# Finishing u one chunk later in the SwiGLU groups of a two-block fp32 transformer kernel, spreading the token sums, and reordering seven products

## The reference, cut to what matters

```python
def _sq_relu_mlp(h, w_up, w_down):          # first block, D_FF = 4096: stages "f0", "f1"
    u = jax.nn.relu(h @ w_up)
    return (u * u) @ w_down

def swiglu(x, w_gu, w_d):                   # second block, D_FF_2 = 2816: "s00", "s01", "s10", "s11"
    gate, up = jnp.split(x @ w_gu, 2, axis=-1)
    return (jax.nn.silu(gate) * up) @ w_d
```

## Time and profile before

| | |
|---|---|
| median of 3 runs | 3586.6 us (3584.88 to 3589.55) |
| profiled execution, its own time | 3591.5 us |
| its span | 3589.8 us |
| TensorE, VectorE, ScalarE, GpSimd busy | 96%, 65%, 40%, 26% of the span |
| mean granted TensorE clock | 0.987 |

### The profile page before, as it was taken

How to read it: one execution, slowest core, us unless ns; L and a number is a source line. 1 busy time by engine, 2 the same in 40 slices (tenths; PEclk the granted TensorE clock), 3 DMA queues, 4 the chain that set the end, 5 groups by cost and what they waited for, 6 DMA issues and landing times. The chain is left out here.

```text
span 3589.8 us, 54969 instructions
## 1 busy us (share of the span) xinstructions
PE 3452.3 (96%) x21523; PEld 2859.4 (80%) x21523; DVE 2330.7 (65%) x3150; ACT 1431.2 (40%) x2021; POOL 950.5 (26%) x635
## 2 busy tenths in 40 slices
PE   8999999999999999999999999999999999999998
PEld 6888888645788878987777788888888777778887
DVE  5655563465866777676577577777777534467776
ACT  5632232464444443333544343344333422244333
POOL 1220011010433225444023054424543000015442
PEclk9999999999999999999999999999999999999999
DMA  3332234100223223222200132223222222212222
GB/s 119 106 109 93 93 94 94 36 1 24 82 94 105 94 86 103 93 94 90 71 26 17 58 106 94 94 83 102 97 93 94 83 82 83 82 63 102 94 94 70
DMA packets 232571, 296.15 MB, mean 82 GB/s; under 512 B 21893, under 2 KB 201464, under 8 KB 232392
## 3 DMA queue, kind: packets, MB, share of 16 engines
q1 hardware_dynamic: 230864, 290.48, 25.0%
q0 software_dynamic: 1152, 3.05, 0.4%
q10 hardware_dynamic: 376, 0.12, 0.0%
HBM read 291.53 MB, written 2.10 MB: 82 GB/s over the span
## 5 line engine op out<-in xcount | busy, mean ns | idle before, releaser
L336 DVE TENSOR_TENSOR wlo<-raw,whi 128x2048 fp32r<-128x2048 f32 x266 | 647.0, 2432 | 336.9 <-ACT whi L330 289.7
L330 ACT ACTIVATE whi<-raw 128x2048 fp32r<-128x2048 f32 x189 | 361.7, 1914 | 705.1 <-PE bank L342 612.7
L340 PE MATMUL bank<-u_hi,whi 128*128 128x512 f32 x1440 | 572.8, 398 | 64.1 <-DVE fsum L819 42.6
L340 PE MATMUL bank<-h_hi,whi 128*128 128x512 f32 (+1 forms) x1516 | 604.6, 399 | 22.9 <-DVE h_lo L1097 11.1
L342 PE MATMUL bank<-h_hi,wlo 128*128 128x512 f32 (+1 forms) x1516 | 590.8, 390 | 0.0
L341 PE MATMUL bank<-h_lo,whi 128*128 128x512 f32 (+1 forms) x1516 | 590.6, 390 | 0.0
L342 PE MATMUL bank<-u_hi,wlo 128*128 128x512 f32 x1440 | 564.0, 392 | 0.0
L341 PE MATMUL bank<-u_lo,whi 128*128 128x512 f32 x1440 | 563.6, 391 | 0.0
L340 PEld LDWEIGHTS bank<-u_hi,whi 128*128 128x128 f32 x1440 | 271.3, 188 | 149.8 <-DVE fsum L819 63.9
L340 PEld LDWEIGHTS bank<-h_hi,whi 128*128 128x128 f32 x1516 | 286.4, 189 | 100.0 <-issue 32.1
L501 PE MATMUL bank<-th,whi 128*128 128x256 f32 x1232 | 345.9, 281 | 0.0
(11 more groups left out here) (487 smaller groups left out, 5982.7 us busy)
## 6 DMA issues: line engine op xcount, KB each, us to landing
raw<-in_ffn_wgu SPq DMA_DIRECT2D x88, 1024.0 KB, 5.0
raw<-in_ffn_wd SPq DMA_DIRECT2D x44, 1024.0 KB, 4.9
raw<-in_mlp_w_up SPq DMA_DIRECT2D x32, 1024.0 KB, 5.4
raw<-in_mlp_w_down SPq DMA_DIRECT2D x32, 1024.0 KB, 4.8
raw<-in_odd_w_in SPq DMA_DIRECT2D x24, 1024.0 KB, 5.1
raw<-in_even_w_in SPq DMA_DIRECT2D x13, 1024.0 KB, 5.3
raw<-in_rg_w_in SPq DMA_DIRECT2D x8, 1024.0 KB, 5.6
raw<-in_odd_w_out SPq DMA_DIRECT2D x8, 1024.0 KB, 5.0
```

Source lines behind the costliest of these rows:

```text
L330: e.activation(whi[:, n % 2, :], raw[:, n % 2, :], ACT.Copy).then_inc(hi_ready, 1)
L336: e.tensor_tensor(wlo[:, n % 2, :], raw[:, n % 2, :], whi[:, n % 2, :].bitcast(F32), ALU.subtract).then_inc(lo_ready, 1)
L340: pe.matmul(o, w_hi, r_hi, start=first, stop=False)
```

## The change

1. u one chunk later: for every product-form group but the last of a stage, the products silu(gate) x up move from the end of the up chunk to the start of the next gate chunk on VectorE (`products`), the u_hi copies on ScalarE behind whi and x_hi of the next group's up chunk (`swi_high`), and u_low out of the down chunk into the next group's gate chunk: behind the last two reads for SwiGLU, ahead of them in f1. x_lo of the next gate chunk moves behind the add of tile 3 in the down chunk.
2. Token sums: in f1 the product form starts at group 5 instead of 3, and the four roundings and remainders stand ahead of groups 2, 3 and 4 (one, two, one). In the SwiGLU stages two stand ahead of gu(2) and two inside it: on ScalarE behind the silus, on VectorE behind the two gate reads, ahead of the wlo of down chunk 1. In f1 the wlo of down chunk 0 is made ahead of `dve_tokens`.
3. The order of the products becomes A, C, B, E, A2, E2, C2; the banks follow.
4. The hardware loop starts one group after the first product-form group.

```diff
-        SEVEN = {"f1": 3, "s00": 3, "s01": 3, "s10": 3, "s11": 3}
+        SEVEN = {"f1": 5, "s00": 3, "s01": 3, "s10": 3, "s11": 3}
...
+            start = SEVEN[name] + 1 if name in SEVEN else 3
+            turns = (G - 1 - start) // 2
...
+            for g in range(1, start):
+                if name in SEVEN and 2 <= g < SEVEN[name]:
+                    between(g)
                 gu(g, n_gu(g), None, 0, 0)
                 dn(g - 1, n_dn(g - 1), None, 0, 0)
...
+        def deferred(name, g):
+            return seven(name, g) and g < FFN[name]["groups"] - 1
...
-        PRODUCTS = (("m", 0, 0, TB11, 0), ("x", XS2, 0, T2, 1), ("x", XS3, 0, T3, 2), ("m", 0, 1, T1, 3),
-                    ("m", 4, 0, TB21, 0), ("m", 4, 1, T4, 2), ("x", XS4, 0, TB22, 3))
-        P_A, P_B, P_E, P_C, P_A2, P_E2, P_C2 = range(7)
+        PRODUCTS = (("m", 0, 0, TB11, 0), ("m", 0, 1, T1, 1), ("x", XS2, 0, T2, 2), ("x", XS3, 0, T3, 3),
+                    ("m", 4, 0, TB21, 0), ("m", 4, 1, T4, 3), ("x", XS4, 0, TB22, 1))
+        P_A, P_C, P_B, P_E, P_A2, P_E2, P_C2 = range(7)
...
+        TOKEN_STEPS = {"f1": {2: (0,), 3: (1, 2), 4: (3,)}}
...
                     act_weights(e, name, g, 1, n + 1, i, dn, dt, lambda: keep(0))
+                    if deferred(name, g - 1):
+                        swi_high(g - 1, i, dt)
...
+            def swi_high(g, i, dt):
+                e.wait_ge(tiles_out, at(after_down(name, g - 2), i, dt))
+                for j in range(2):
+                    e.wait_ge(prod_done, at(2 * (bs + g) + 2, i, 4))
+                    e.activation(u_hi[:, 2 * (g % 2) + j, :], tmp[:, 2 + j, :], ACT.Copy).then_inc(uhi_done, 1)
...
                         e.activation(tmp[:, j, :], tmp[:, j, :], ACT.Silu).then_inc(silu_done, 1)
+                    if g == 2 and name in SEVEN:
+                        act_tokens(e, name, (2, 3))
...
                 if f["swiglu"]:
+                    if deferred(name, g - 1):
+                        products(g - 1, i)
                     dve_lo(e, n + 1, i, dn, dt)
                 joined(0)
                 last_quarter(0)
                 if f["swiglu"]:
                     dve_weights_rest(e, name, g, 1, n + 1, i)
+                elif deferred(name, g - 1):
+                    u_low(g - 1, i)
                 outer(0, P_E2, tmp[:, 1, LEFT], gate_done)
                 outer(0, P_C2, tmp[:, 0, RIGHT], gate_done)
                 if not f["swiglu"]:
                     return
+                if deferred(name, g - 1):
+                    u_low(g - 1, i)
                 dve_lo(e, n + 2, i, dn, dt)
...
+                if not deferred(name, g):
+                    products(g, i)
+
+            def products(g, i):
+                d0 = dve7_base[name] + 8 * (g - SEVEN[name])
                 e.wait_ge(silu_done, at(2 * (bs + g) + 1, i, 4))
...
                 if f["swiglu"]:
+                    if g == 2 and name in SEVEN:
+                        dve_tokens_rest(e, name, (2, 3))
                     if g > 0:
                         dve_lo(e, n + 2, i, dn, dt)
...
                 u_low(g, i)
-                if g == 0:
-                    if name in SEVEN:
-                        dve_tokens(e, name, stage)
                 if g == 0 and not f["swiglu"]:
                     dve_lo(e, n + f["gu"] + 1, i, dn, dt)
+                if g == 0 and name in SEVEN:
+                    dve_tokens(e, name, stage)
...
-                    if m == first + 2 and seven(name, g + 2):
+                    if m == (4 if early else 6) and seven(name, g + 2):
                         dve_weights_rest(e, name, g + 2, 0, n + 1, i)
-                    if m == 3 and early:
+                    if m == 3 and early and not deferred(name, g + 1):
                         u_low(g + 1, i)
```

More of the change, by code:

```diff
@@ L383, in chunk_down, with ffn_walk @@
             return where[name] + G * (gu + 1) - 1 if g == G - 1 else where[name] + gu + g * (gu + 1) + gu
-        def ffn_walk(e, name, gu, dn, between=lambda: None):
+        def ffn_walk(e, name, gu, dn, between=lambda g: None):
             f = FFN[name]
@@ L393, in n_dn @@
                 return chunk_down(name, g)
[L394 to L397, removed]
+            start = SEVEN[name] + 1 if name in SEVEN else 3
+            turns = (G - 1 - start) // 2
+            dt = before[n_gu(start + 2)] - before[n_gu(start)]
             gu(0, n_gu(0), None, 0, 0)
-            for g in (1, 2):
-                if g == 2 and name in SEVEN:
-                    between()
+            for g in range(1, start):
+                if name in SEVEN and 2 <= g < SEVEN[name]:
+                    between(g)
                 gu(g, n_gu(g), None, 0, 0)
                 dn(g - 1, n_dn(g - 1), None, 0, 0)
-            with e.Fori(0, turns - 1) as i:
-                for g in (3, 4):
+            with e.Fori(0, turns) as i:
+                for g in (start, start + 1):
                     gu(g, n_gu(g), i, 2 * per, dt)
                     dn(g - 1, n_dn(g - 1), i, 2 * per, dt)
-            for g in range(2 * turns + 1, G):
+            for g in range(start + 2 * turns, G):
                 gu(g, n_gu(g), None, 0, 0)
@@ L411, in ffn_walk, with token_steps @@
             dn(G - 1, n_dn(G - 1), None, 0, 0)
+        def token_steps(name, g):
+            return TOKEN_STEPS[name][g] if name in TOKEN_STEPS else (0, 1)
+        def deferred(name, g):
+            return seven(name, g) and g < FFN[name]["groups"] - 1
         def after_down(name, g):
@@ L478, in pe_seven @@
                     pe.wait_ge(xlo_ready, at(y + 1, i, k))
-                if p <= P_C and c == 0:
+                if p < 4 and c == 0:
                     free(p)
@@ L498, in pe_seven @@
                         hi, lo = x_hi[:, s, q, j, :], x_lo[:, s, q, j, :]
-                    first = j == 0 and p <= P_C
+                    first = j == 0 and p < 4
                     last = j == 3
@@ L527, in pool_tokens, with act_tokens, dve_tokens_rest @@
                 e.tensor_tensor(v[T4], v[TB21], v[T2], ALU.subtract).then_inc(t_sum, 1)
-        def act_tokens(e, name):
+        TOKEN_STEPS = {"f1": {2: (0,), 3: (1, 2), 4: (3,)}}
+        def act_tokens(e, name, ks):
             z = t_no[name]
-            for k in range(4):
+            for k in ks:
                 e.wait_ge(t_sum, 8 * z + 4 * (k // 2) + 4)
                 e.activation(th[:, k, :, 1, :], th_raw[:, k, :, 0, :], ACT.Copy).then_inc(t_hi, 1)
-        def dve_tokens_rest(e, name):
+        def dve_tokens_rest(e, name, ks):
             z = t_no[name]
-            for k in range(4):
+            for k in ks:
                 e.wait_ge(t_hi, 4 * z + k + 1)
@@ L630, in gu_seven @@
                 weights(g + 1, n + f["gu"] + 1, i, dn, dt)
+                if f["swiglu"]:
+                    if not deferred(name, g):
+                        swi_high(g, i, dt)
+                    return
                 e.wait_ge(tiles_out, at(after_down(name, g - 2), i, dt))
@@ L633, in gu_seven @@
                     u = 2 * (g % 2) + j
[L634 to L641, removed]
+                    e.wait_ge(ulo_done, at(2 * (b + g - 1) + j + 1, i, 4))
+                    e.wait_ge(seven_act, at(a0 + 4, i, 2 * acts))
+                    e.activation(tmp[:, 2 + j, :], tmp[:, j, :], ACT.Square)
+                    e.activation(u_hi[:, u, :], tmp[:, j, :], ACT.Square).then_inc(uhi_done, 1)
+            def swi_high(g, i, dt):
[3 more added lines that the diff above has]
+                    e.activation(u_hi[:, 2 * (g % 2) + j, :], tmp[:, 2 + j, :], ACT.Copy).then_inc(uhi_done, 1)
             def gu(g, n, i, dn, dt):
@@ L677, in act_ffn @@
                 e.preload_act_table(ACT.Silu)
-            ffn_walk(e, name, gu, down, lambda: act_tokens(e, name))
+            ffn_walk(e, name, gu, down, lambda g: act_tokens(e, name, token_steps(name, g)))
         def pool_ffn(e, name):
@@ L694, in down @@
                 pass
-            ffn_walk(e, name, gu, down, lambda: pool_tokens(e, name))
+            ffn_walk(e, name, gu, down, lambda g: pool_tokens(e, name) if g == 2 else None)
         def dve_ffn(e, name, stage):
@@ L748, in gu_seven @@
                 outer(1, P_C2, tmp[:, 2, RIGHT], seven_dve)
+                if not deferred(name, g):
+                    products(g, i)
+            def products(g, i):
+                d0 = dve7_base[name] + 8 * (g - SEVEN[name])
                 e.wait_ge(silu_done, at(2 * (bs + g) + 1, i, 4))
-                step(7)
+                e.wait_ge(seven_dve, at(d0 + 7, i, 16))
                 e.tensor_tensor(tmp[:, 3, :], tmp[:, 3, :], tmp[:, 1, :], ALU.mult).then_inc(prod_done, 1)
                 e.wait_ge(silu_done, at(2 * (bs + g) + 2, i, 4))
-                step(8)
+                e.wait_ge(seven_dve, at(d0 + 8, i, 16))
                 e.tensor_tensor(tmp[:, 2, RIGHT], tmp[:, 2, RIGHT], tmp[:, 0, RIGHT], ALU.mult).then_inc(prod_done, 1)
@@ L827, in down @@
                     dve_lo(e, n + 2, i, dn, dt)
```

(2 more changed lines are left out.)

## The result

| | before | after |
|---|---|---|
| median of 4 runs on one chip | 3587.2 us (3584.88 to 3589.55) | 3550.62 us (3549.62 to 3555.46) |
| profiled execution | 3591.5 us | 3549.62 us |
| mean granted TensorE clock | 0.987 | 0.989 |

The ratio is 0.9901 [0.9884, 0.9918], faster by 1.0%. The forecast was 3547.0 in 3518 to 3572. The profiled executions differ by 41.9 us, the medians by 36.6; the sum of the prediction was 39.6.

The account below looks back on a forecast made before the run. TensorE is busy 96%, so only its waits and number of matmuls can move the time. The sum -64.2 + 18.5 + 16.8 - 10.7 = -39.6 from the 3586.6 us median gives 3547.0 us, range 3518 to 3572.

Parts of the forecast that it names:

- Work leaving the down chunk: SwiGLU down chunks: products and u_lo leave, x_lo moves behind tile 3's add; all 2.3 us lost in each go, -64.2 us.
- The turns: From gate chunk start G, VectorE's u_lo and wlo alternate with GpSimd's sums; the up chunk's sixth product waits, +18.5 us.
- Rival (1): No turns lost: up chunks wait for nothing, the SwiGLU stage start costs only 0.35 us; 3513 us, chance 0.17.
- In 28 up chunks: Count of SwiGLU up chunks whose sixth product waits, 0.66 us each with the restart, +18.5 us.
- Order of the products: Product C second: gain 0, but the fourth product's bank is wanted 1.41 us after the product ends instead of 2.83.
- This is what lets the 0.66 appear: Claim that the new product order's narrower space permits the up chunk's sixth product loss of 0.66 us.
- Start of a SwiGLU stage: Two token remainders ahead of down chunk 1's wlo: TensorE waits 2.7 us, clock loses 1.4; 4.2 a stage, +16.8 us.
- the up chunk's sums that were to end about G: GpSimd's four sums for the up chunk end about G instead of 4 us ahead; smallest margin, no price.
- f1: Stage f1: +2.0 for two plain groups, -6.5 in down chunks, -6.2 from spread token remainders; together -10.7 us.
- the 4 us wait: f1's 4.03 us wait for wlo at 945.03: freed there, about as long at tile 4 instead; 0, at best -4.
- -6.2 + 2.0: f1: spreading token remainders saves 6.2 us at down chunk 1; making groups 3 and 4 plain costs 2.0.

Follow-up runs that it names:

- experiments 4 and 5: Each against the kernel after: 4, products back at the end of their own up chunk, 3549.01 us; 5, x_lo back ahead of tile 3's add, 3550.28 us.
- experiment 1: Kernel after, with the two u_lo of SwiGLU groups ahead of the last two gate reads instead of behind them; 3531.15 us.
- experiment 7: Kernel after, with u_lo ahead of the last two gate reads and all four SwiGLU token remainders ahead of group 2; 3513.29 us.
- experiment 2: Kernel after, with the products in the old order A, B, E, C, A2, E2, C2 and its banks; 3551.63 us.
- Experiment 3: Kernel after, with all four token roundings and remainders of the SwiGLU stages ahead of group 2, as before the change; 3535.11 us.
- experiment 6: Kernel after, with f1's product form from group 3 again and its four token remainders in one piece ahead of group 2; 3552.42 us.
- experiment 8: On top of experiment 7, token products made in two halves in all five stages, two of four pairs later; 3526.53 us.

## Why the prediction was right, and where it was not

**Work leaving the down chunk: right.** 64.2 was read from the earlier trace rows; 64.5 was there and 0.8 is left. But of the three things that leave or move, the products and x_lo are worth nothing by themselves (experiments 4 and 5); what is left is u_lo.

**The turns: right, and the heart of it.** The prediction laid out, from G, the ends of sum, u_lo, sum, u_lo, sum, wlo at 11.18, 11.72, 12.88, 13.42, 14.58 and 16.75. The rows of the group give 11.16, 12.86 and 14.57 for the sums, 13.41 for the second u_lo, 16.72 for wlo. TensorE's sixth product, due at G+16.96, starts at 17.56, 0.6 us late, plus a restart of 0.1. The rule that the prediction cited from the Trainium skill, page "SBUF — State Buffer", section "Who interferes with whom", by which such instructions shut each other out whole, agrees with these rows; experiment 1 is the test, since u_lo out of the sums' way takes 1.28 us instead of 2.98. Rival (1), where no turn is lost, is refuted for this kernel. Its mechanism was seen in one of the 24 chunks: in the second product-form group of s01 (G = 2178.40) the first sum began at G+11.17 instead of 9.86, both u_lo were through in 1.28 us, and the up chunk waited for nothing. What rival (1) promised, 3513, is what experiment 7 reached by moving the work.

**How many up chunks wait: wrong by four.** "In 28 up chunks" counted group 10 of each stage, which has a u_lo to finish but no further gate chunk, so no sums beside it. It is 24, of which one (s01) had no wait; the mean is 0.74 instead of 0.66. The two misses partly cancel, which is luck: 16.9 for 18.5.

**Order of the products: wrong.** "This is what lets the 0.66 appear" is refuted by experiment 2. The step looked at when the product ends, and the read was held by VectorE's wlo.

**Start of a SwiGLU stage: right.** Two remainders were to take 5.4 us and wlo 3.3, with TensorE 2.7 late; it was 5.39 and 3.37, and 2.8 in each of the four stages; the sums beside them alternate with them (1342.72, 3.07 us for a sum of 1.3). The clock was off: 1.4 in each stage was forecast, from a row behind a wait of 2.04 us, and it is 1.7 in three and 0.1 in s01. The prediction's 2.7 and 1.4 make 4.1, not 4.2; the total of 16.4 for 16.8 is so near because a dearer clock in three stages meets almost none in the fourth.

**First gate chunk: missing.** In s01 and s11 the sums of that chunk's partner, each drawn out by a VectorE instruction (3.41 and 2.79 in the rows above), end so late that ScalarE's whi and VectorE's wlo follow late, and the gate chunk's sixth product waits. The prediction had named this margin, the up chunk's sums that were to end about G, as its smallest, and priced it at nothing; in s01 they end at G+3.04. It looked for a wait at a sixth product only in up chunks. Experiment 3 shows that it hangs on the two remainders.

Why s00 and s10 escape is in the traces. From the start D of down chunk 1, the next gate's wlo comes at D+6.35 in s01, where the clock stayed at 1.00: it gets in behind the first of the four sums, and the sums end at D+14.03. In s00 the lower clock makes VectorE wait for TensorE's tiles, wlo comes at D+7.95, behind the third sum, and the sums end at D+12.35, with the gate chunk itself 1.6 us later. In s11 the clock fell too, but the sums began at D+6.55 instead of 5.0. In the 24 stage starts of after and of experiments 1, 2, 4, 5 and 6, the gate chunk lost 1.05 to 2.72 us in all 11 where down chunk 1 ran at full clock, and lost only in 2 of the 13 where it did not, both with late sums.

**f1: right.** -10.6 for -10.7; the 4 us wait moved from the start of down chunk 0 to its tile 4, as said, with 1.5 us of lower clock behind it. The parts fit as well: down chunk 1 lost 6.3 before and loses nothing now. But experiment 6 shows that the later start of the product form is worth 1.6 us, not the 4.2 that -6.2 + 2.0 makes: without it 3.6 is lost there, where the four remainders took 11.12 us instead of 12.23 and the clock stayed up. What shortened them was not tested.

## What to carry to other kernels

Work that has to be moved off a late engine should go where the engine that it takes turns with is still, not merely where its own timeline has a gap: the gap of 1.52 us here was beside GpSimd's sums and cost 17 us, the place 2 us earlier, two short reads ahead, was free. Before spreading a burst of work over several places, ask of each place what is due behind it: the burst ahead of group 2 had cost TensorE nothing in the SwiGLU stages (from its first weight matmul to down chunk 1, s00 took 80.90 us before and 83.65 after, with the new wait of 2.8 in it), while its second half ahead of a wlo cost 16 us. When a change has several parts, test each alone; here the move of u_lo is what is left to explain nearly all of the gain, the new order and the moves of products and x_lo were worth nothing, and the spreading in the SwiGLU stages cost 16 us.

## What the runs showed of the hardware that was not expected

- Turns between VectorE and GpSimd are not always one for one. In the groups each sum got in behind the next VectorE instruction, but in experiment 8 one addition took 7.14 us, where the next ones took 1.28, through wlo and two remainders that VectorE ran without a gap; it did so in all four stages. What makes it lose three turns stays open.
- The granted clock after equal waits was not equal: after 2.63 us at 1351.11 it was 0.86 over the next chunk, some matmuls at 1.2 GHz and the rest at 2.4, and after 2.63 us at 2103.75 it was 1.00. Over the 24 stage starts named above, all with this wait (2.62 or 2.63 us), the chunk behind it lasted 12.56 to 12.63 us in 13 and 10.98 to 11.01 in 11. The wait costs 4.5 us in s00 and 2.9 in s01, but s01 loses 1.35 of the difference again in its first gate chunk.
- A wait of TensorE costs some 0.1 us more than it lasts: behind each wait at a sixth product the next matmul starts 0.1 us later than its spacing of 0.1177.
